# Half of the token tiles through the mixer first, the other half between their experts, and a different split of the value rows

## The reference

```python
h_l = modulate(rmsnorm(x_lat, g_pre_mix), sh1_l, sc1_l)          # h_c likewise from ctx
mix_l, _ = token_mixer(h_l, h_c, ...)
x_lat = x_lat + gt1_l * rmsnorm(mix_l, g_post_mix)
h2_l  = modulate(rmsnorm(x_lat, g_pre_ffn), sh2_l, sc2_l)
x_lat = x_lat + gt2_l * rmsnorm(peer(h2_l, w_q, keys, u, v), g_post_ffn)
# token_mixer: proj = h @ w_in  ->  z, xbc, dt, g_b, g_c, v
#   SSD part:   y = bidirectional state-space scan of conv(xbc); y * silu(z), normed in 4 groups
#   short conv: rmsnorm(g_b * conv3(g_c * v))
#   out = concat(SSD part, short conv) @ w_out
# peer, per token and per head (8 heads, 128 x 128 product keys):
#   q = h @ w_q;  s = q . keys;  top 16 of each side;  top 16 of the 256 sums -> expert ids, softmax g
#   act = gelu(<u[eid], h>);   out = sum over 128 experts of g * act * v[eid]
```

## Time and profile before

| | |
|---|---|
| device time, median of 3 runs | 2147.56 us (2145.64 to 2148.24) |
| profiled execution, its own time | 2150.96 us |
| its span, first to last instruction | 2149.2 us |
| busy: PE / DVE / ACT / POOL | 1539.9 / 1489.6 / 473.9 / 906.1 us |
| first and last gather issued | 731.2 and 2124.3 us |

### The profile page before, as it was taken

One profiled execution on the slowest core, in us unless ns is written; L12 is line 12 of the kernel. 1 busy time (PEld: TensorE's weight loads), 2 busy tenths in 40 slices (PEclk: granted clock), 3 DMA queues, 4 the chain that ended last, 5 costly groups with the idle time before them and its releaser, 6 DMA issues.

```text
span 2149.2 us, 15031 instructions
## 1 busy us (share of the span) xinstructions
PE 1539.9 (72%) x4280; PEld 800.9 (37%) x4280; DVE 1489.6 (69%) x2861; ACT 473.9 (22%) x1383; POOL 906.1 (42%) x658
## 2 busy tenths in 40 slices
PE   6799999999899677787654556555555555555555
PEld 2465785554588554455211111111111111111111
DVE  1555307665802675657798898898898898888976
ACT  2200120000201322222222222223222222322222
POOL 2568400321200143333555455555456455555553
PEclk9799799999999898999777776777677677777777
DMA  9334221111344488988999999999999999999997
GB/s 317 119 108 149 76 79 39 40 39 59 118 136 144 172 299 333 345 318 316 374 397 376 416 402 423 408 405 389 409 416 401 398 421 387 392 422 412 410 421 296
DMA packets 140470, 622.05 MB, mean 289 GB/s; under 512 B 11132, under 2 KB 68708, under 8 KB 74852
## 3 DMA queue, kind: packets, MB, share of 16 engines
q0 software_dynamic: 78880, 556.83, 65.1%
q1 hardware_dynamic: 59872, 64.03, 9.2%
q10 hardware_dynamic: 1636, 0.23, 0.1%
HBM read 618.95 MB, written 2.10 MB: 289 GB/s over the span
## 4 chain that ended last, share of the span: by engine, by line
DMA 23%; PE 17%; DVE 13%; issue 6%; ACT 4%; POOL 3%; ACTq 0%; POOLq 0%
DMA arena<-in_peer_uv,arena 23%; PE bank L835 11%; DVE arena L1486 5%; PE bank L806 5%; POOL arena L550 3%; DVE arena L1501 3%; ACT smalls L1046 1%; ACT arena L1041 1%; PE bank L824 1%; ACT arena L1036 1%; DVE arena L1446 1%; ACT arena L1022 0%; ACT arena L1018 0%; DVE smalls L1453 0%; PE bank L816 0%
## 5 line engine op out<-in xcount | busy, mean ns | idle before, releaser
L835 PE MATMUL bank<-arena,smalls 128*128 128x512 f32 x1024 | 732.1, 855 | 529.4 <-ACT smalls L1046 529.4
L550 POOL DMA_INDIRECT arena<-in_peer_uv,arena x512 | 702.4, 1372 | 839.6 <-DVE arena L1501 470.1
L1486 DVE CUSTOM_DVE_ANT_0 arena<-arena 128x1024 f32<-128x1024 f32 x512 | 617.0, 1221 | 93.4 <-DMA arena<-in_peer_uv,arena 92.9
L835 PEld LDWEIGHTS bank<-arena,smalls 128*128 128x128 f32 x1024 | 231.8, 249 | 997.0 <-ACT smalls L1046 784.1
L1501 DVE SCALAR_TENSOR_TENSOR arena<-arena 128x1024 f32<-128x1024 f32 x252 | 322.1, 1278 | 153.2 <-ACT arena L1041 153.2
L606 PE MATMUL bank<-arena 128*128 128x512 f32 (+1 forms) x832 | 327.2, 551 | 3.5 <-ACT arena L885 3.2
L1036 ACT ACTIVATE arena<-arena 128x2 f32<-128x2 f32 x256 | 51.9, 203 | 840.9 <-DVE arena L1486 839.4
L606 PEld LDWEIGHTS bank<-arena 128*128 128x128 f32 x832 | 158.4, 192 | 154.6 <-issue 145.3
L1041 ACT ACTIVATE arena<-arena 128x1 f32<-128x1 f32 x512 | 122.9, 287 | 8.6 <-ACT arena L1036 0.2
L806 PE MATMUL bank<-arena 128*128 128x256 f32 x512 | 122.4, 395 | 2.3 <-issue 2.3
L806 PEld LDWEIGHTS bank<-arena 128*128 128x128 f32 x512 | 103.7, 203 | 34.5 <-issue 21.0
(11 more groups left out here) (223 smaller groups left out, 1296.3 us busy)
## 6 DMA issues: line engine op xcount, KB each, us to landing
arena<-in_w_in SPq DMA_DIRECT2D x24, 1024.0 KB, 5.5
arena<-in_w_ada POOLq DMA_DIRECT2D x16, 1024.0 KB, 5.9
arena<-in_w_out SPq DMA_DIRECT2D x16, 1024.0 KB, 4.9
arena<-in_w_ada SPq DMA_DIRECT2D x8, 1024.0 KB, 11.3
arena<-in_peer_w_q SPq DMA_DIRECT2D x8, 1024.0 KB, 7.0
arena<-in_peer_uv,arena POOLq DMA_INDIRECT x512, 8.8
arena<-in_x SPq DMA_DIRECT2D x4, 512.0 KB, 12.3
arena<-in_x POOLq DMA_DIRECT2D x1, 2048.0 KB, 8.1
```

The source lines that it names most:

```text
L550: nc.gpsimd.indirect_dma_start(gslot[n % NGS], None, uv_tab[0], bass.IndirectOffsetOnAxis(eid[t % 2][:, k:k + 1], 0)).then_inc(s_gsl[n % N ...
L835: last = mm(acc[h][:, :], diag[:, j % NDG], row_v(n)[:, h * 512:(h + 1) * 512], start=(i == 0), stop=(i == BT - 1))
L1486: V.tensor_tensor_reduce(row_u(n), row_u(n), h2[:, t], 1.0, 0.0, ALU.mult, ALU.add, dots[:, k:k + 1]).then_inc(s_dot, 1)
```

## The change

Three things. First, tiles 0 and 1 go through the mixer alone: `z`, the 24 projections, the group norms, `yT` and `wo` are done for them only (256 tokens instead of 512), then their norms, and the experts begin. The scan itself (`step`, `r`, `y`, `off`, `out`) is still done for all four tiles ahead of that. Second, the other half of that work stands in `BSEQ` behind the `pk` steps, a piece to a step (`late`), between the query units of tiles 0 and 1 and those of tiles 2 and 3. Third, of four gathered rows DVE adds one (`n % 4 == 0`) and TensorE three, where it was two and two.

```diff
-    plan += [("z", hq, m) for hq in range(4) for m in range(LT)]
+    plan += [("z", hq, 0) for hq in range(4)]
...
+    on_dve = [n % 4 == 0 for n in range(NPK)]
+    row_no = [sum(d == on_dve[n] for d in on_dve[:n]) for n in range(NPK)]
...
+    for hq in range(4):
+        add(2 * hq, ("z", hq, 0))
+        add(2 * hq + 1, ("z", hq, 1))
+        add(2 * hq + 2, ("zy", hq))
+    add(9, ("gs", NA))
...
+    for n, (kind, ct) in enumerate(projs):
+        add(8 + n, ("proj", n))
+        if kind == "v":
+            add(9 + n, ("conv", ct))
+        elif kind == "gb":
+            add(9 + n, ("gate", ct))
+            add(10 + n, ("sq", ct))
+            add(11 + n, ("sqa", ct))
...
+    for i in range(16):
+        add(n + i, ("wo", i // 4, i // 2 % 2, i % 2))
+        if i % 4 == 3:
+            add(n + i + 1, ("mix", i // 4))
+    n += 17
+    for i, kind in enumerate(("n1", "n2", "n3", "n4")):
+        add(n + 2 * i, (kind, NA))
+        add(n + 2 * i + 1, (kind, NA + 1))
+
+    side = [s for u in units[2:NUA] for s in unit_steps(u)]
+    side += late
+    UB = 88
+    side += [[] for _ in range(UB - len(side))]
+    side[UB - 2].append(("h2T", NA))
+    side[UB - 1].append(("h2T", NA + 1))
+    side += [s for u in units[NUA:] for s in unit_steps(u)]
...
-        if j in (0, 2):
-            BSEQ.append(("h2T", 2 + j // 2))
-        u = 2 + j // 3
-        if u < len(units):
-            BSEQ += unit_steps(units[u])[j % 3]
+        if j < len(side):
+            BSEQ += side[j]
...
+        mixer_loads(0)
+        query_loads(0)
+        mixer_loads(1)
+        query_loads(1)
...
-                        pool.wait_ge(s_peused, (n - NGS) // 2 + 1)
+                    if on_dve[n - NGS]:
+                        pool.wait_ge(s_vadd, row_no[n - NGS] + 1)
                     else:
-                        pool.wait_ge(s_vadd, (n - NGS) // 2 + 1)
+                        pool.wait_ge(s_peused, row_no[n - NGS] + 1)
...
-                A(diag[:, j % NDG], ident[:], ACT.Copy, scale=wexp[:, k + 1:k + 2]).then_inc(s_diag, 1)
+                for i in range(2):
+                    r = row_no[2 * j + i]
+                    if not on_dve[2 * j + i]:
+                        if r >= NDG:
+                            act.wait_ge(s_peused, r - NDG + 1)
+                        A(diag[:, r % NDG], ident[:], ACT.Copy, scale=wexp[:, k + i:k + i + 1]).then_inc(s_diag, 1)
```

More of the change, by code:

```diff
@@ L53, in build @@
     WRING = 4
+    NA = LT // 2
+    HS = NA * P
+    halves = (range(NA), range(NA, LT))
     plan = ["rowsA", ("ada1", 0), "rowsB"] + [("ada1", g) for g in range(1, 4)] + ["ada1T"]
@@ L179, in build @@
             qring.append(step)
+        elif step[0] == "z" and step[2] == 0:
+            qring.append(("z", step[1], 1))
+        elif step[0] == "proj":
+            qring.append((*projs[step[1]], 1))
+        elif step[0] == "yT":
+            qring += [("yT", step[1], h) for h in range(2)]
+        elif step[0] == "ss":
+            qring.append(("ss", 1))
+        elif step[0] == "wo" and step[3] == 0:
+            qring.append((*step[:3], 1))
     for n, name in enumerate(qring):
@@ L975, in norms, with sc_drain @@
-            def norms(tp):
-                a, b = 2 * tp, 2 * tp + 2
-                for m in range(a, b):
-                    A(h2[:, m], mix[m], ACT.Square, accum_out=mss[:, m:m + 1]).then_inc(s_mss, 1)
+            def sc_drain(nq, half):
+                ps = await_bank(act, ("wo", nq, 1, half))
+                if nq >= 2:
+                    await_read(act, ("wo", nq - 2, 0, half))
+                for i, m in enumerate(halves[half]):
+                    last = A(sBt[:, nq % 2, i * WCOL:(i + 1) * WCOL], ps[:, i * WCOL:(i + 1) * WCOL], ACT.Copy,
+                             scale=scss[:, m:m + 1])
+                release(last, ("wo", nq, 1, half))
@@ L985, in norms, with x1_root @@
+            def x1_root(half):
+                a, b = half * NA, half * NA + NA
                 act.wait_ge(s_xss, b)
                 A(xrs[:, a:b], xss[:, a:b], ACT.Sqrt, bias=epsc[:, 0:1], scale=1.0 / D).then_inc(s_xr, 1)
-            sc_part(0)
-            norms(0)
-            sc_part(1)
+            for m in halves[0]:
+                y_drain(m)
+            act.wait_ge(s_scn, 2)
+            for nq in range(4):
+                sc_drain(nq, 0)
+            await_read(act, ("wo", 3, 0, 0))
@@ L991, in _ @@
+            for m in halves[0]:
+                A(h2[m], mix[m], ACT.Square, accum_out=mss[:, m:m + 1]).then_inc(s_mss, 1)
+            mix_root(0)
+            for m in halves[0]:
+                x1_squares(m)
+            x1_root(0)
             for q4 in range(NQ // 4):
@@ new lines, in modulated @@
+            def modulated(m):
+                if m % NA == 0:
+                    dve.wait_ge(s_xr, m // NA + 1)
+                    link(V.reciprocal(xrs[:, m:m + NA], xrs[:, m:m + NA]))
+                link(V.scalar_tensor_tensor(out=h2[m], in0=x1t[m], scalar=xrs[:, m:m + 1],
+                                            in1=rows[ROW_SC2], op0=ALU.mult, op1=ALU.mult))
+                V.tensor_tensor(h2[m], h2[m], rows[ROW_SH2], ALU.add).then_inc(s_h2, 1)
+            sc_sum(0)
+            for ct in range(NX):
+                last = V.tensor_scalar(scT[0][:, ct], scT[0][:, ct], colA[:, A_SG + ct:A_SG + ct + 1], None, ALU.mult)
@@ L1388, in after @@
+            last.then_inc(s_scn, 1)
+            for m in halves[0]:
+                group_scale(m)
+            sc_inverse(0)
+            for m in halves[0]:
+                y_drain(m)
+            for nq in range(4):
+                wo_drain(nq, 0)
+            for m in halves[0]:
+                add_mix(m)
+            for m in halves[0]:
+                modulated(m)
             def after(step):
```

582 lines of the change are left out of this document (344 added, 238 removed).

## The result

The changed kernel takes 2217.84 us (median of 4 runs, 2215.93 to 2219.82), the kernel before, run beside it, 2147.9 us: a ratio of 1.0325, 95% interval 1.0307 to 1.0343. It is 70 us slower; 2129 us was forecast. The profiled execution took 2219.8 us, its span is 2218.1.

What follows compares the result with a forecast made beforehand. TensorE mainly bounds the mixer, and gather transfers nearly alone the plain expert steps. Ahead of the first gather -143, in the steps +124, net -19: span 2130, 2129 us as median, range 2072 to 2190.

Steps and rivals of the forecast that it cites:

- Ahead of the first gather, -143: Mixer stretch before the expert steps: halved work brings the first gather from 731.2 to 588 us, bounds -165 and -120.
- Query thirds, +0.86 a step: 42 expert steps with thirds of query units: TensorE's extra half row is paid in full, +36 us.
- Late projections and `wo`, 6.95: 40 expert steps with late products: engines' 6.5 to 6.6 and transfers' 6.65 us give 6.95 a step, +70 us.
- late steps in series: Rival: the 48 steps with late products take 7.7 us, plain steps stay at 5.21; 2175 us, chance 0.30.
- Late `z`, 7.6: Eight expert steps with late `z`: copy in series and table load in each second step, 7.6 us each, +19 us.
- Twelve other steps, 6.1: Expert steps with `yT`, sums and late norms: more DVE and ACT work and table switches, 6.1 us each, +11 us.
- 118 plain steps, 5.21 to 5.11, and 36 at 5.03: Plain expert steps: 118 with search gain from earlier slots, -12 us; 36 without search stay unchanged, 0.
- the 0.18 us: Plain expert step: its time above the transfers alone (5.21 against 5.03 us), put down to slots DVE gives back late.
- the upper bound (+50): Slow-side bound on the 118 plain steps with search, whose forecast was -12 us.
- my own sign of a wrong mechanism: Stated sign of a wrong mechanism: first gather later than 611 us, or plain steps slowed.
- TensorE bounds the plain steps: Rival: rows at 1.2 GHz make TensorE limit the plain steps, 5.67 us each; 2200 us, chance 0.07.

Runs made afterwards that it cites:

- experiment 1: Changed kernel, but VectorE adds two rows of four again and TensorE two, mixer split and late work kept: 2099.4 us, ratio 0.9763.
- Experiment 10: Kernel of experiment 1 with its 24 late loads cut to one eighth of their data (tiles 2 and 3 computed with incomplete weights): 2096.74 us, ratio 0.9754.
- experiment 11: Changed kernel with late `z` of tiles 2 and 3 copied instead of passed through silu: 2206.53 us, ratio 1.0263.
- experiments 4 and 13: Changed kernel, three of four rows kept on TensorE, with ten gather slots (2149.49 us) or seven (2154.83 us) instead of six from row 240 on.

## Why the prediction was wrong

- *Ahead of the first gather, -143.* Right: 141, and not by luck: `wo` begins 97 us earlier (592.0 to 495.0; 100 forecast), takes 55 us less, and from its end to the first gather it is 11 us more (12 forecast).
- *Query thirds, +0.86 a step.* Right in direction, high by 0.17 and 0.40 us. Against the kernel of experiment 1 the third row measured 0.45 and 0.42 us there, half of what I charged. I had charged it on the mean of 6.82; the first 18 such steps took 7.09 us before and 7.06 in experiment 1, the other 24 took 6.70 and 6.86.
- *Late projections and `wo`, 6.95.* The sum held (7.21 and 6.52), the reason did not. I had let the transfers set 6.65 of it and charged 48 half loads at 1.62 us, 78 us. Experiment 10 took seven eighths of them away for 3 us, or 9 by its profile. So of the two demands that I set beside each other, 6.5 to 6.6 us of engines and 6.65 of transfers, taking most of the loads out of the second moved the steps by only 0.1 to 0.3 us (on the kernel of experiment 1); that the sum came out is in part luck. The "late steps in series" rival may have had the mechanism, with the wrong price (7.7).
- *Late `z`, 7.6.* Mis-sized: 8.58. I counted one table load in two steps at its own 1.28 us, which is the right count; but it is paid once as a pause and again as a row at the lower clock level (experiment 11), and the third row beside late `z` costs 1.29 us a step (7.29 to 8.58) where 0.86 was charged. *Twelve other steps, 6.1*: `yT` took 8.3.
- *118 plain steps, 5.21 to 5.11, and 36 at 5.03.* This is the step that failed: the 144 steps behind the queries took 5.63 us where 5.09 was forecast on average, +77 of the 89 us between forecast and result, and with it the sign. "DVE has one L1501 (1.3 us) less in two steps and gives slots back earlier" was not true: the row that VectorE kept is done 0.3 us later, and only TensorE's first row of the four 0.3 us earlier. I read POOL's 186 us on VectorE as the cause of the 0.18 us and did not ask what the slot of the moved row now waits for: its diagonal and 3.2 us on TensorE, and the next row behind it 4.2 us more, 1.3 us on average over all slots. I gave the upper bound (+50) to another mechanism, and gave the 36 steps without search nothing at all; they lost 0.3 us each. Slower plain steps were my own sign of a wrong mechanism, and it came.
- *The rival "TensorE bounds the plain steps"* named 5.67 us a step, 5.66 was measured, and it is refuted: in experiments 4 and 13 TensorE added 13 and 11% more rows in the same time at a granted clock of 0.86 and 0.87, with steps of 5.05 and 5.08 us. A rival can hit the number for the wrong reason. The clock did rise in the changed kernel, from 0.75 to 0.81 in the stretch above, as the prediction said against this rival, and the steps slowed all the same; PE was busy 66% of it and not the 85% that I worked out, since a matmul of a row fell from 879 to 771 ns and the steps grew.

Not settled: how the 54 us of the third row in the late steps divide between slots and engines in series (no spare room was found there for a slot), what sets the late steps, and how the extra price of rows in pairs divides. Their slots are held 1.4 us longer with six slots; the traces put a good half of it ahead of the dot products, but whether VectorE's own pair does that, and how the pause and the clock behind it share the rest, was not taken apart by a run.

## What to carry to other kernels

Before moving work off an engine that returns buffers late, write the buffer's round: slots times pace, landing, hold. If slots x the bare transfer time (here 6 x 2.51 = 15.1 us) is already below the round (15.6), a microsecond that a move adds to the hold lengthens the round, whatever the engines' busy shares say: here 1.3 us of hold made it 16.9. Then count the slots before the balance: a seventh gave back 63 us with the worse split, two rows of four gave back 118, and with both two of four and ten slots it was 133. A change with two independent parts should be priced as two: the mixer split was worth -48 us, and the row split +118 on top of it.

## What was not expected of the hardware

- With three rows of four and seven slots the median from issue to landing was 9.9 us at 411 GB/s, with ten 17.0 us at 416: three more gathers in flight did little but lengthen the landing.
- Seven eighths of 24 loads of 1.049 MB, beside gathers at a DMA share of 1.00, cost 3 us together by the medians and 9 by the steps of the profiles, though at the queue's own 3.24 us a load they are 68. At a share of 1.00 that stretch moved 390 GB/s, while the ten-slot kernels moved 416 to 421 at 1.01: a share near 1 was no proof that transfers set the pace.
- With two rows of four on TensorE a matmul of a row took 887 ns when they came one by one and 905 in pairs, at granted clocks of 0.74 and 0.70: bunching them did not lift the clock. The pauses ahead of them grew as well, from 248 us ahead of 111 rows to 282 ahead of 49 pairs.
